# Where the next stage's weights are negated, the log table loaded, and a recurrence's variance summed

## What is computed

```python
for l in range(DEPTH):                                  # first_block
    h = rms_norm(x, norm1_w[l]) * (1.0 + sc1) + sh1
    x = x + g1 * hybrid_mixer(h, w_in[l], w_out[l], ...)
    h = rms_norm(x, norm2_w[l]) * (1.0 + sc2) + sh2
    x = x + g2 * conv_ffn(h, w_gate[l], w_val[l], ..., w_down[l])
x = rms_norm(x, final_norm_w)
for i in range(DEPTH):                                  # second_block
    proj = rmsnorm(x, norm_mix_pre) @ w_in
    y_att = sliding_window_attention(rope(q), rope(k), v, sinks) @ w_o_att
    y_rw = rwkv7_time_mix(rw, ...) @ w_o_rw
    x = x + rmsnorm((sigmoid(gate_a) * y_att + sigmoid(gate_b) * y_rw) @ w_out, norm_mix_post)
    x = x + rmsnorm((gelu(ua) * ub) @ w_down, norm_ffn_post)
    x = x + rmsnorm(sigmoid(x @ w_ple_gate) * (p_i @ w_ple), norm_ple)
```

## Time and profile before

| what | us |
|---|---|
| median of three runs | 4455.27 (4441.81 to 4456.62) |
| the profiled execution | 4447.68 |
| its span | 4445.8 |
| TensorE busy | 3942.4 (89%) |
| VectorE busy | 2143.0 (48%) |
| ScalarE busy | 1723.3 (39%) |
| GpSimd busy | 791.4 (18%) |

### The profile page before, as it was taken

One profiled execution on the slowest core, in us unless ns is written; L12 is line 12 of the kernel. 1 busy time (PEld: TensorE's weight loads), 2 busy tenths in 40 slices (PEclk: granted clock), 3 DMA queues, 4 the chain that ended last, 5 costly groups with the idle time before them and its releaser, 6 DMA issues.

```text
span 4445.8 us, 70148 instructions
## 1 busy us (share of the span) xinstructions
PE 3942.4 (89%) x29148; PEld 3156.2 (71%) x29148; DVE 2143.0 (48%) x3621; ACT 1723.3 (39%) x2512; POOL 791.4 (18%) x1108
## 2 busy tenths in 40 slices
...
DMA packets 189741, 628.75 MB, mean 141 GB/s; under 512 B 22768, under 2 KB 27888, under 8 KB 189040
## 3 DMA queue, kind: packets, MB, share of 16 engines
q0 software_dynamic: 158976, 549.52, 57.2%
...
...
## 4 chain that ended last, share of the span: by engine, by line
PE 43%; DVE 9%; ACT 6%; DMA 3%; issue 2%; ACTq 0%; POOL 0%; DVEq 0%; SPq 0%
PE bank L214 10%; PE bank L215 10%; PE bank L216 10%; PE bank L1922 5%; PE bank L1885 1%; ACT L2078 1%; ACT at_s L1505 1%; ACT w_lo L154 1%; ACT w L2078 1%; PE bank L1983 1%; PE bank L1911 1%; PE bank L1981 1%; DVE rw_z L2340 1%; ACT gate L2078 1%; DVE at_s L1696 1%
## 5 line engine op out<-in xcount | busy, mean ns | idle before, releaser
L214 PE MATMUL bank<-h_hi,w_hi 128*128 128x512 f32 x2576 | 1067.0, 414 | 90.1 <-DMA w_lo<-in_b_wq 33.3
L215 PE MATMUL bank<-h_lo,w_hi 128*128 128x512 f32 x2576 | 1025.2, 398 | 0.0
L216 PE MATMUL bank<-h_hi,w_lo 128*128 128x512 f32 x2576 | 1023.9, 397 | 0.0
L154 ACT ACTIVATE w_lo<-w_hi 128x1024 fp32r<-128x1024 f32 (+2 forms) x552 | 556.0, 1011 | 1175.0 <-DMA w_hi<-in_a_wgv 326.2
L214 PEld LDWEIGHTS bank<-h_hi,w_hi 128*128 128x128 f32 x2576 | 489.3, 190 | 240.8 <-issue 118.0
L215 PEld LDWEIGHTS bank<-h_lo,w_hi 128*128 128x128 f32 x2576 | 489.2, 190 | 118.1 <-issue 10.8
L216 PEld LDWEIGHTS bank<-h_hi,w_lo 128*128 128x128 f32 x2576 | 487.9, 189 | 119.4
L2078 ACT ACTIVATE gate<-bank 128x512 f32<-128x512 f32 x80 | 47.8, 597 | 274.6 <-PE bank L1922 274.6
L1365 DVE TENSOR_SCALAR fa_conv<-fa_a_in,par_a 128x512 f32<-128x512 f32 x44 | 21.6, 492 | 242.2 <-ACT fa_a_in L1312 242.0
L214 PE MATMUL bank<-fa_y_hi,w_hi 128*128 128x512 f32 x352 | 137.3, 390 | 1.2 <-DMA w_lo<-in_a_wd 1.2
L214 PE MATMUL bank<-fb_y_hi,w_hi 128*128 128x512 f32 x352 | 137.1, 389 | 0.1
...
## 6 DMA issues: line engine op xcount, KB each, us to landing
w_hi<-in_a_wgv POOLq DMA_DIRECT2D x80, 512.0 KB, 5.4
w_lo<-in_a_wgv POOLq DMA_DIRECT2D x80, 512.0 KB, 7.7
w_hi<-in_b_wup POOLq DMA_DIRECT2D x80, 512.0 KB, 5.2
w_lo<-in_b_wup POOLq DMA_DIRECT2D x80, 512.0 KB, 7.4
w_hi<-in_a_wh POOLq DMA_DIRECT2D x48, 512.0 KB, 4.7
w_lo<-in_a_wh POOLq DMA_DIRECT2D x48, 512.0 KB, 5.7
fa_ada_raw<-in_ada SPq DMA_DIRECT2D x48, 512.0 KB, 7.4
w_hi<-in_b_wrkv POOLq DMA_DIRECT2D x48, 512.0 KB, 4.3
```

The costliest lines, as they stand in the source:

```text
L154: st.do(st.eng.activation(self.lo[:, s], self.hi[:, s].bitcast(F32), ACT.Copy, scale=-1.0), (self.neg_made, n + 1))
L214: pe.matmul(out, self.hi[:, a], hh[:, k0 + k, :], start=first and k == 0, stop=False)
L215: pe.matmul(out, self.hi[:, a], hl[:, k0 + k, :], start=False, stop=False)
L216: mm = pe.matmul(out, self.lo[:, a], hh[:, k0 + k, :], start=False, stop=last and k == ks - 1)
```

## The change

Nothing is computed that was not computed before, except one more one-column Ln per pair of the recurrence. The parts:

1. `released(st, used)` negates those of the next stage's first pieces whose place in the ring is free once `used` pieces are used. The output loops of mixer_a, mix_b and ple_b call it after each square but the last; ffn_a and ffn_b call it once, before the last square. The calls of `first_pieces(early)` go. The one-column Ln of `act_rstd` becomes `act_ready` and stands before the last square.
2. In mix_b, ple_b and final_norm_a, two pieces behind `head` are negated after the squares of part 1, with `act_ready` before them, ahead of `act_rstd`. In ffn_a they are negated before `sc.enter`.
3. In ple_b the eight first pieces are negated at four places instead of two. In attention_b unit 22 is negated before `act_again`, and unit 23 after its fourth step.
4. The shuffles of attention_b are issued by SyncE.
5. In the output loops VectorE's addition of the square before stands ahead of its work on the new tile.
6. In rwkv_b, w takes bank 2 and ssq and the c products bank 3; the variance is summed ahead of the k projection, and its Ln and Exp stand before `first_exps`; the Ln table is loaded after the square of k, and the Exp for rt follows the one for the norm. On VectorE the bonus' input goes to `kp`, rt is made after at_, with a semaphore of its own (`rt_made`), the bonus multiply moves behind step 6, `ec` and bbar behind step 3, and one mask of xt ahead of the last `keep_masked`.

```diff
@@ -194,6 +194,13 @@
+def released(self, st, used):
+    own = self.ring.pieces[self.base:self.base + self.count]
+    count = sum(before <= used for _, _, _, before, _ in own)
+    if count:
+        self.first_pieces(st, count)
@@ -324,11 +331,14 @@
+def act_ready(self, st):
+    st.settle()
+    st.do(st.eng.activation(self.run.spare[:, 0:1], self.run.eps[:, 0:1], ACT.Ln))
...
     run = self.run
-    st.settle()
-    st.do(st.eng.activation(run.spare[:, 0:1], run.eps[:, 0:1], ACT.Ln))
     self.wait(st.eng, "sum", part + 1)
@@ -422,14 +432,13 @@
-def act_again(self, st, scale):
+def act_again_one(self, st, k, scale):
     run = self.run
-    for k in range(KD):
-        self.wait(st.eng, "xn", k + 1)
-        st.settle()
-        st.do(st.eng.activation(run.hh[:, k, :], run.w[:, k % 3, :], ACT.Identity, scale=scale[:, k:k + 1]),
-              self.sig("hi", k + 1))
+    self.wait(st.eng, "xn", k + 1)
+    st.settle()
+    st.do(st.eng.activation(run.hh[:, k, :], run.w[:, k % 3, :], ACT.Identity, scale=scale[:, k:k + 1]),
+          self.sig("hi", k + 1))
@@ -578,6 +587,7 @@
         edge.act_square(st, k, run.x[:, k, :])
+    edge.act_ready(st)
     nxt.first_pieces(st, 2)
@@ -861,9 +871,11 @@
         if n == KD - 1:
-            nxt.first_pieces(st, nxt.early)
+            after.act_ready(st)
         after.wait(act, "x", n + 1)
         after.act_square(st, n, x[:, n, :])
+        if n < KD - 1:
+            nxt.released(st, ws.last[first_out + n])
     st.settle()
@@ -1242,12 +1254,12 @@
     for n in range(KD):
+        if n:
+            after.dve_acc(st, n - 1)
         dve.wait_ge(*ws.done(first_out + n + 1))
...
                                        in1=x[:, n, :], op0=ALU.mult, op1=ALU.add), after.sig("x", n + 1))
-        if n:
-            after.dve_acc(st, n - 1)
     st.settle()
@@ -1301,6 +1313,7 @@
             ws.first_pieces(st, 8)
+    ws.high(st, 4)
     sc.enter(act)
@@ -1318,7 +1331,8 @@
         if n == KD - 1:
-            nxt.first_pieces(st, nxt.early)
+            nxt.released(st, ws.last[2 * KF + 3 * n])
+            after.act_ready(st)
         after.wait(act, "x", n + 1)
@@ -1490,6 +1504,13 @@
     sp.dma_start(sink[:, :], io["b_sink"][l]).then_inc(const_in, 16)
+    for nr in range(2 + KD):
+        b = nr % 2
+        sp.wait_ge(p_free, nr + 1)
+        for q in range(4):
+            sp.dma_start(sw[32 * q:32 * q + 32, b, :], raw[32 * (q ^ 1):32 * (q ^ 1) + 32, b, :])\
+                .then_inc(sw_in[b], 16)
     sc.leave(sp)
@@ -1543,11 +1564,6 @@
             st.do(act.activation(raw[:, b, :], bank_of(i)[:, :], ACT.Copy), (p_free, i + 1))
-            st.settle()
-            for q in range(4):
-                act.dma_start(sw[32 * q:32 * q + 32, b, :], raw[32 * (q ^ 1):32 * (q ^ 1) + 32, b, :])\
-                    .then_inc(sw_in[b], 16)
             nr += 1
@@ -1561,7 +1577,11 @@
             sigmoid_steps(st, mixed[:, m, :], mixed[:, m, :], (ga_made, m + 1), half)
-    again.act_again(st, gain)
+    ws.high(st, 21)
+    for k in range(KD):
+        again.act_again_one(st, k, gain)
+        if k == 3:
+            ws.high(st, 22)
     ws.high(st, 27)
@@ -1806,7 +1826,7 @@
 sq_made, ssq_made, rn_made, rk_made = sc.sem("sq_made"), sc.sem("ssq_made"), sc.sem("rn_made"), sc.sem("rk_made")
-at_made, bon_made = sc.sem("at_made"), sc.sem("bon_made")
+at_made, rt_made, bon_made = sc.sem("at_made"), sc.sem("rt_made"), sc.sem("bon_made")
 bbar_made, kbar_made = sc.sem("bbar_made"), sc.sem("kbar_made")
@@ -1823,11 +1843,12 @@
 for p in range(PAIRS):
-    wide = [("w", p, 3, p_free), ("a", p, 5, p_free)]
-    order += (wide if p else []) + [("k", p, 0 if p else 1, p_free)] + ([] if p else wide)
+    wide = [("w", p, 2, p_free), ("a", p, 5, p_free)]
+    order += wide if p else []
     if p >= 2:
         order.append(("var", p - 2, 4, pn_free))
-    order += [("r", p, 1 if p else 0, p_free), ("ssq", p, 2, pd_free), ("v", p, 0 if p else 1, p_free),
+    order += [("k", p, 0 if p else 1, p_free)] + ([] if p else wide)
+    order += [("r", p, 1 if p else 0, p_free), ("ssq", p, 3, pd_free), ("v", p, 0 if p else 1, p_free),
               ("g", p, 1 if p else 0, p_free), ("bonus", p, 5, pd_free)]
@@ -1855,7 +1876,7 @@
 def gate_bank(m):
-    return banks[(3, 5, 2, 4)[m % 4]]
+    return banks[(2, 5, 3, 4)[m % 4]]
@@ -1928,20 +1949,20 @@
             if p:
-                pe.wait_ge(f_free, 5 * p - 1)
+                pe.wait_ge(f_free, 5 * p)
                 pe.wait_ge(x_made, 5 * p)
...
         if p:
-            decays()
-        ws.project(pe, claim("k", p), hh, hl)
-        if p == 0:
             decays()
...
             whole("var", p - 2, bones[:, :], yq[:, :], var_made)
+        ws.project(pe, claim("k", p), hh, hl)
+        if p == 0:
+            decays()
         ws.project(pe, claim("r", p), hh, hl)
@@ -1954,18 +1975,20 @@
         pe.wait_ge(rk_made, p + 1)
-        whole("bonus", p, bones[:, :], r, bon_made)
+        whole("bonus", p, bones[:, :], kp, bon_made)
...
             pe.wait_ge(at_made, p + 1)
+            pe.wait_ge(*read("w", p))
+        elif j == 1:
             pe.wait_ge(*read("ssq", p))
-        elif j == 1:
-            pe.wait_ge(*read("w", p))
         else:
             pe.wait_ge(f_free, f - 1)
+        if j == 3:
+            pe.wait_ge(rt_made, p + 1)
         products(2 + j % 2, lhs, rhs_, f_made)
@@ -1990,8 +2013,8 @@
         else:
-            pe.wait_ge(f_free, 5 * p + 5)
-        products(2, ct, xx, cx_made)
+            pe.wait_ge(f_free, 5 * p + 4)
+        products(3, ct, xx, cx_made)
@@ -2050,7 +2073,7 @@
             whole("var", PAIRS - 1, bones[:, :], yq[:, :], var_made)
-    pe.wait_ge(f_free, 5 * PAIRS - 1)
+    pe.wait_ge(f_free, 5 * PAIRS)
     pe.wait_ge(x_made, 5 * PAIRS)
@@ -2135,6 +2158,9 @@
             decays(p)
+            if p >= 2:
+                log_var(p - 2)
+                rstd(p - 2)
             first_exps(p)
@@ -2146,21 +2172,17 @@
             first_exps(p)
-        if p >= 2:
-            log_var(p - 2)
         if p:
...
         do(e0, ks, ACT.Square, scale=col("k_k", p), signal=(sq_made, p + 1))
-        if p >= 2:
-            rstd(p - 2)
+        do(run.spare[:, 0:1], run.eps[:, 0:1], ACT.Ln)
         copy_out("r", p, f + 1, n + 1)
-        act.wait_ge(ssq_made, p + 1)
-        do(e0, cum, ACT.Exp, signal=(eb_made, p + 1))
-        ws.high(st, n + 3)
         act.wait_ge(*read("ssq", p))
...
         do(kn, kn, ACT.Exp, scale=-0.5, bias=run.eps[:, 1:2], signal=(rn_made, p + 1))
+        do(e0, cum, ACT.Exp, signal=(eb_made, p + 1))
+        ws.high(st, n + 3)
         copy_out("v", p, f + 2, n + 2)
@@ -2184,7 +2206,7 @@
                 act.wait_ge(xcxt_made, q)
-            do(pp, banks[2][:, :], ACT.Copy, signal=(cx_kept, q + 1))
+            do(pp, banks[3][:, :], ACT.Copy, signal=(cx_kept, q + 1))
             if i < 2:
@@ -2307,9 +2329,7 @@
         shift(f + 1, "r", p, r, col("mu_r", p))
-        dve.wait_ge(eb_made, p + 1)
-        do(dve.tensor_tensor(rt[b], r, e0, ALU.mult))
-        do(dve.scalar_tensor_tensor(out=r, in0=r, scalar=col("r_k", p), in1=kp, op0=ALU.mult, op1=ALU.mult),
+        do(dve.scalar_tensor_tensor(out=kp, in0=r, scalar=col("r_k", p), in1=kp, op0=ALU.mult, op1=ALU.mult),
            (rk_made, p + 1))
@@ -2318,9 +2338,9 @@
            (at_made, p + 1))
+        dve.wait_ge(eb_made, p + 1)
+        do(dve.tensor_tensor(rt[b], r, e0, ALU.mult), (rt_made, p + 1))
         shift(f + 2, "v", p, v, col("mu_v", p))
-        dve.wait_ge(bon_made, p + 1)
-        do(dve.tensor_tensor(bonus[:, b, :], bank("bonus", p)[:, :], v, ALU.mult), read("bonus", p))
@@ -2352,17 +2372,19 @@
         step(3)
+        do(dve.tensor_copy(ec[:, b, :], e0[:, C - 1:S:C]))
+        ends = ec[:, b, :].unsqueeze(2).broadcast_to([P, NC, C])
+        do(dve.tensor_tensor(chunks(e0), chunks(a), ends, ALU.mult), (bbar_made, p + 1))
         keep_masked(2)
...
         step(5)
+        do(dve.tensor_tensor(chunks(xt[b]), chunks(mabt), each_chunk(lm[:, 3, :]), ALU.mult))
         keep_masked(4)
-        do(dve.tensor_tensor(chunks(xt[b]), chunks(mabt), each_chunk(lm[:, 3, :]), ALU.mult))
         step(6)
         do(dve.tensor_tensor(chunks(xt[b]), chunks(xt[b]), one, ALU.add), (xt_made, 6 * p + 1))
-        do(dve.tensor_copy(ec[:, b, :], e0[:, C - 1:S:C]))
-        ends = ec[:, b, :].unsqueeze(2).broadcast_to([P, NC, C])
-        do(dve.tensor_tensor(chunks(e0), chunks(a), ends, ALU.mult), (bbar_made, p + 1))
+        dve.wait_ge(bon_made, p + 1)
+        do(dve.tensor_tensor(bonus[:, b, :], bank("bonus", p)[:, :], v, ALU.mult), read("bonus", p))
         step(7)
@@ -2436,9 +2458,11 @@
         if m == KD - 1:
-            nxt.first_pieces(st, nxt.early)
+            edge.act_ready(st)
         act.wait_ge(*ws.done(KD + m + 1))
         edge.act_square(st, m, banks[m % 2][:, :])
+        if m < KD - 1:
+            nxt.released(st, ws.last[KD + m])
     edge.act_rstd(st)
@@ -2446,6 +2470,8 @@
```

(28 more changed lines are left out.)

4 lines of the change are left out of this document (2 added, 2 removed).

## The result

The changed kernel takes 4346.6 us (median of four runs, 4342.3 to 4357.8) beside 4453.9 for the kernel before. The ratio is 0.9768, with a 95% interval of 0.9742 to 0.9794: 103 to 107 us less, where 171 were forecast. The direction was right and the size was not. The forecast lay at 4284. The profiled execution was the longest of the four, 4357.8 us (span 4356.0).

What follows compares the result with a forecast made beforehand. TensorE, busy 3942.4 of 4445.8 us, was taken as the bound, with its waits at stage seams the main loss. Savings 41.6 + 83.6 + 24.0 + 22 = 171 off 4447.7, plus 7.6 to the runs' median, gave 4284; range 4240 to 4350.

Steps and rivals of the forecast that it cites:

- C: attention: output weights negated earlier save 21.0 us, shuffles issued by SyncE save 3.0; bounds 15 and 29.
- A: Seams between stages: earlier negations of streamed weights let the last square and closing sum run sooner, saving 41.6 us.
- B: Stage openings (ffn_a, ffn_b, attention, ple_b): landed weights waiting for ScalarE are negated sooner, saving 83.6 us.
- some 10: ffn_b's opening: with the negation before rstd, TensorE resumes some 10 us sooner than before the change.
- the output weights: attention: output weights negated ahead of the affine steps, 10.5 us saved in each layer, 21.0 in all.
- D: Recurrence: shorter TensorE waits save 43 us, a new front of variance work costs 20.5; net 22 saved.
- the steady gain: Recurrence: 3.1 us saved per period, less 1.7 charged in the 12 periods with p >= 2.
- 1: Rival, recurrence front: none of the 3.8 us of table loads, Ln and Exp is hidden; 4314 us, chance 0.15.
- 2: Rival, mix_b and ple_b loops: squares wait for loads while TensorE needs their bank; 84 us lost, 4368, chance 0.11.
- 3: Rival, seams: the clock comes back wholly after the long stalls; 25 us more saved, 4259, chance 0.10.
- 4: Rival, mix_b and ple_b loops become serial, 8.3 us more per unit, 232 lost; slower than before, 4516, chance 0.03.
- 5: Rival, seams: loads, not their negations, set them, so 27 us less is saved; 4311, chance 0.08.

Runs made afterwards that it cites:

- e2: The kernel before with only one part of the change, the attention_b shuffles issued by SyncE: 4471.7 us, ratio 1.0045.
- e1: The changed kernel with the four attention_b shuffles issued by ScalarE again, all else as changed: 4325.3 us, ratio 0.9709.
- e7: The changed kernel with the Ln table loaded ahead of the output loops' last negations in mixer_a, ffn_a, mix_b and ffn_b: 4341.9 us, ratio 0.9756.
- e4: The changed kernel with the whole of rwkv_b as it was before, all else as changed: 4368.1 us, ratio 0.9813.
- g3: The kernel before, with ffn_a's layer 0 modulation weights from the fourth piece on fetched as 64 KB instead of 512 KB: 4443.8 us, ratio 0.9986.

## Why the prediction was wrong

The step that failed is the shuffles' in C: -3 put in, and some +20 (e2) to +28 (e1's profiles) measured, 35 of the 80 us that the profiles lack. With the shuffles back on ScalarE (e1) the kernel takes 4325.3, still 41 above the forecast, and the terms of A and B below make up 27 of that in the profiles.

- **A** (41.6, bounds 15 and 55): 32.4 at its seams. The chain was read rightly, and mix_b and ple_b came within 1 us. The two mixer_a seams gave 6.7 for 15. There two more negations, each behind its load, follow TensorE's last products, and the table load is on the path (1.5, e7); I costed it at nothing, because it was hidden in before.
- **B** (83.6, bounds 60 and 95): 65.5. Attention's share was right (27.2 for 26.1). ple_b gave 11.8 for 25: I took the in_b_p wait as unchanged at the sum, where it reappears behind it, and dated the gate weights by their landing in before, although their places come free only behind that product. ffn_a and ffn_b gave 26.5 for 32.5. In ffn_a of layer 0 I didn't ask what else had lain under the stall (VectorE's sums, 4.5 us). In ffn_b the first whole unit does start 10.8 and 11.0 us sooner, as my "some 10", but 3.9 and 2.3 of it go again in the next units, in new waits for w_lo and on VectorE (L2621).
- **C**: the output weights were right (24.2 for 21). For the shuffles the bounds of C left room for some 6 the other way. I checked what is queued on SyncE and that ScalarE has slack. I didn't ask what ScalarE does with the 2.5 us that it gains. It negates, and that releases a 512 KB load into the shuffles. The issues on ScalarE had kept them apart.
- **D** (22, bounds -20 and 43): 23 by e4. The sum came out by luck, for its parts were wrong: the steady gain (0.39 a period) is a fourth of that put in, and the first two pairs, called even, bring 12 of the 20 that the profiles show.
- **Rivals.** 1 is out (e4). 2 shows as ScalarE's waits in the loops, but no TensorE wait of over 2 us stands in the output loops of mix_b or ple_b. 3, 4 and 5 didn't come about. The parts of 4's serial unit add up to 7.1 to 7.6, not to the 8.3 that it was charged at; nothing hangs on it. None of the five was a collision of transfers, so the range ended at 4350, just where the time came to lie.
- Open: the start of mixer_a is 0.2 to 8.2 us later in the profiles of changed kernels than in before, mostly some 3, though nothing but the prologue's table load is changed ahead of it. Of the two kernels without that change e2 isn't later and g3 is by 2.0, so part of it is scatter. No run tells the cause.
